# A Strassen-style gated MLP in six groups of weight chunks: 3, 4, 4, 4, 4, 3 instead of 2, 4, 4, 4, 4, 4, with new orders on ScalarE and VectorE

## The chip, the cores and the metric

The kernel runs on one core of one Trainium2 chip. The metric is the device time of one execution in microseconds. Before the change it is 1894.84 us, the median of 3 runs (1894.76 to 1895.4). All times below are microseconds unless marked ns.

## The reference, cut to what matters

The program is one inference step of a two-layer encoder over 656 tokens: 16 meta tokens, 512 prompt frames and 8 x 16 sample frames. Each layer has a token mixer (left untouched here) and then the channel mixer, in float32:

```python
def conv_ffn(h, p, buf):
    u = h @ p['w_ffn_up']                      # 1024 -> 2 x 2816
    a, v = u[..., :D_FF], u[..., D_FF:]
    ext = jnp.concatenate([buf.astype(a.dtype), a], axis=1)
    c = p['ffn_conv_b'] + sum(ext[:, j:j + T] * w[j] for j in range(CONV_W))
    out = (jax.nn.silu(c) * v) @ p['w_ffn_down']   # 2816 -> 1024
    return out, ext[:, -(CONV_W - 1):]
```

Its output is normalised (RMSNorm) and added to x, and the next layer begins with another norm.

## The kernel before, in words

Tokens lie along the free dimension (656 = 2 halves of 328), channels on the 128 partitions. D_FF = 2816 makes 22 chunks of 128 channels, c0 to c21. Every float32 product is done as three matmuls of 328 columns, on operands split in a high and a low part. ScalarE (ACT) makes the high part of a piece of weights (whi), VectorE (DVE) the low part (wlo, whi subtracted from the raw weights); both also do all the elementwise work, and each runs strictly in the order that is written for it.

**Plain chunks.** Chunks 0 to 2 (NPL = 3) compute a and v as ordinary tiles. TensorE (PE) computes tiles T_UP to T_UP + 5; on DVE `plain_a`, `conv_rest`, `plain_v` and `g_low` turn them into the gated product g, split in gh and gl. Meanwhile ACT and DVE form the sums of activations that the Strassen chunks need: Sh/Sl and part of Hh/Hl (`s_sum`, `s_high`, `s_low`).

**Strassen chunks.** Chunks 3 to 21 use seven products each (B11, B21, T2, T3, T1, T4, B22) of 12 matmuls (`chunk`, L928 on PE, L1970 on ACT, L2773 on DVE). ACT copies partial results out of PSUM: p1 after B11, u2 after T2, p7 after T3. T2 needs p1 taken, T1 needs u2 taken, T4 needs p7 taken, and B22 needs DVE's addition of T1 to p7 (`dve_took`). Beside its own products, the chunk's ACT and DVE orders finish the previous chunk, called pending: `conv_first`, `conv_rest`, `silu`, `times_v`, `g_high`, `g_low`. In the last group `times_v` also multiplies by R.

**Down passes.** GROUPS (L65) says after which chunks a down pass comes. A pass over a group of nk chunks (`down_pass`, L977) computes 8 output tiles n, each nk blocks of 6 matmuls, in three PSUM banks (G0, WB, G1). For n = 0 to 2 it first runs all blocks but those of the last chunk. In the first pass ACT copies the tiles to Y; in later ones DVE adds them to Y. The last pass runs n = 3 to 7 in halves of the tokens, all first halves first, so that the norm of the first half can begin (`norm_sum_a`).

**The weight stream.** Pieces of 512 KB are loaded by SP's queue into four slots (`raw_slot`, L257; wraw holds 0 and 1, wff 2 and 3), each once the piece that held the slot has been split. The Strassen sums of weights T1 to T4 are made by GpSimd's (POOL's) accumulating DMAs (L731 to L760), in one order: within a group T1 of chunk c + 1 is issued ahead of T4 of chunk c. T1 of c + 1 waits for that chunk's v piece to be loaded, T4 of c for the split of B21 of c. Split weights go into a ring of three full slots; `split_after` (L502) lists, for each product or piece of the stream (a unit), which splits may be made once it has been computed, and `highs(l, u)` (L1581) and `lows(l, u)` (L2259) make all those that are listed up to unit u. T4 and B22 are mostly split as one pair.

Of the kernel before, what the change touches and what calls it, by code (L numbers as in the profile page):

```python
# [18 lines left out]
ALU = mybir.AluOpType  # L19
# [5 lines left out]
KD = D // P  # L25
# [15 lines left out]
KF = FF // P  # L41
# [20 lines left out]


NPL = 3
GROUPS = [(0, 2), (2, 6), (6, 10), (10, 14), (14, 18), (18, KF)]  # L65
NQ = len(GROUPS)
NS = KF - NPL
G4 = 4
# [6 lines left out]

def group_of(c):
    return next(q for q, (c0, c1) in enumerate(GROUPS) if c0 <= c < c1)

# [27 lines left out]
def build(nc, a):  # L108
# [6 lines left out]
    with ctx:  # L115
# [126 lines left out]
        def chunk_no(l, c):  # L242
            return l * NS + c - NPL
# [11 lines left out]
            return u if q is None else P_PASS[q] + u - U_PASS[q]  # L255

        def raw_slot(p):  # L257
            return p % 2 if p < P_UP + 2 * NPL else p % 4

        def raw_of(p):  # L260
            return wraw[:, p % 2, :] if raw_slot(p) < 2 else wff[:, p % 2, :]

        def last_unit(p):

# [236 lines left out]

        split_after = {}  # L502
        _i = P_UP + 2 * NPL - 1
        for _u in range(U_PROD[NPL], UNITS_L):
            _w, _k = max(users[UNITS_L + _u]) - UNITS_L, product_of(_u)
            if _k and product_of(_w):
                _w += LATE[_k[1]]
            _i = max(_i, _w)
            split_after.setdefault(_i, []).append(_u)
# [71 lines left out]
        def _(sp):  # L581
# [32 lines left out]
            for g in range(DEPTH * PIECES):  # L614
# [28 lines left out]
                p = g % PIECES  # L643
                if earlier[g] is not None:
                    sp.wait_ge(S("w_split"), earlier[g] // PIECES * UNITS_L + last_unit(earlier[g] % PIECES) + 1)
                if p == P_CHUNK[NPL]:
                    sp.wait_ge(S("oas_taken"), l + 1)
                    sp.wait_ge(S("ob_split"), HG * (l + 1))
                    sp.wait_ge(S("out"), 32 * (l + 1))
# [147 lines left out]
        def _(pe):  # L797
# [130 lines left out]
            def chunk(l, c):  # L928


                j, s, q = chunk_no(l, c), c % 2, group_of(c)
                x_, y_, z_ = bank(G[s], 0), bank(G[s], 1), bank(WA, s)
                lo, hi = slice(0, KH), slice(KH, KD)
                a_, b_ = cols_of(0), cols_of(1)
# [533 lines left out]
        def _(act):  # L1468
# [13 lines left out]
            def f(*args, **kw):  # L1482
                prev()
                return act.activation(*args, **kw)  # L1484
# [108 lines left out]
            for l in range(DEPTH):  # L1593
# [376 lines left out]
                def chunk(c, pending):  # L1970


                    u0, s = U_PROD[c], c % 2

                    def after(i):
                        act.wait_ge(S("product"), product_no(l, c, i))

                    if pending is not None:
                        conv_first(pending)
                        carry(pending)  # L1980
                    highs(l, u0 - 1)
                    after(B11)
                    act.wait_ge(S("ax"), l * KF + c)
                    did(f(p1, bank(G[s], 0), ACT.Copy), "act_took")
                    highs(l, u0 + B11)
                    if pending is not None:
                        silu(pending)
                    halo(c)
                    highs(l, u0 + B21)
                    after(T2)  # L1990
                    did(f(u2, bank(G[s], 0), ACT.Copy), "act_took")
                    highs(l, u0 + T2)
                    if pending is not None:
                        g_high(pending)
                    after(T3)
                    act.wait_ge(S("gl"), 2 * (l * KF + c) - 1)
                    did(f(p7[:, :], bank(WA, s), ACT.Copy), "act_took")
                    highs(l, u0 + T1)
                    highs(l, u0 + T4)

                for q, (c0, c1) in enumerate(GROUPS):
                    for c in range(max(c0, NPL), c1):
                        chunk(c, c - 1 if c > max(c0, NPL) else None)
                    last_c, u0, nk = max(c1 - 1, NPL - 1), U_PASS[q], c1 - c0
                    if q:
                        conv_first(last_c)
                        carry(last_c)
                        highs(l, u0 - 1)
                        silu(last_c)
                    else:  # L2010
                        highs(l, u0 - 1)
                    g_high(last_c)
                    if q == NQ - 1:
                        w_high(l, UNITS_L - 1)
                    for n in range(KD):
                        if not q:
                            act.wait_ge(S("down"), down_no(l, q, n))
                            did(f(two(Y[:, n, :]), halves(down_bank(n)), ACT.Copy), "act_took")
                        if not q and n == 3:
                            s_high(Sh[:, 0, :, :], Sf[:, 0, :, :], 18)  # L2020
                            act.wait_ge(S("tile"), t0 + T_UP + 2 * NPL)
                            for x in range(2):
                                s_high(Hh[:, 2 * x:2 * x + 2, cols_of(1)], s4_part(x), 12, -1.0)
                        if q < NQ - 1 and nk * (n + 1) % 8 == 0:
                            highs(l, u0 + nk * (n + 1) // 8 - 1)
                exp_table()
                split_to[0] = 0
# [82 lines left out]
                    act.dma_start(a["o_conv"][l], cout[:, :, :]).then_inc(S("conv_out"), 16)  # L2110
                else:
                    rstd_post_a(2 * l + 2)
                    square(0, 0)
                    square(0, 1)
                    for n in (3, 4):
                        ffn_out_b(n)
                        scale_y(n, 1)
                    ffn_out_b(KD - 3)
                    scale_y(KD - 3, 1)
                    ffn_out_b(KD - 2)  # L2120
                    scale_y(KD - 2, 1)
                    ffn_out_b(KD - 1)
                    square(0, 2)
                    square(0, 3)
                    rstd_post_b(2 * l + 2)
# [23 lines left out]
        def _(dve):  # L2149
# [173 lines left out]
            for l in range(DEPTH):  # L2323
# [398 lines left out]
                def times_v(c):  # L2722
# [5 lines left out]
                    if group_of(c) == NQ - 1:  # L2728
                        step(tt_(d, d, R[:, :], ALU.mult))
                    dve.wait_ge(S("product"), product_no(l, c, B22))  # L2730
                    did(stt(d[:, cols_of(0)], bank(G[c % 2], 0), -1.0, d[:, cols_of(0)], ALU.mult, ALU.mult), "dve")
                    did(stt(d[:, cols_of(1)], p7[:, :], -1.0, d[:, cols_of(1)], ALU.mult, ALU.mult), "gl")

                def s_low(i, to, src, hi_, scale=1.0):
# [26 lines left out]
                plain_v(1)  # L2761
                plain_a(2)
                w_low(l, P_UP + 6)
                g_low(1)
                conv_rest(2)
                plain_v(2)
                w_low(l, P_UP + 7)
                for k in range(KH):
# [3 lines left out]

                def chunk(c, pending):  # L2773

                    u0, s = U_PROD[c], c % 2
                    s_ = ax[:, c % 2, :]

                    def after(i):
# [2 lines left out]
                    lows(l, u0 - 2)  # L2781
                    if pending is not None:
                        conv_rest(pending)
                    lows(l, u0 + B11)
                    after(B21)
                    dve.wait_ge(S("act_took"), act_took(l, c, 0))
                    step(tt_(s_[:, 2:2 + HALF], bank(G[s], 1), p1, ALU.add))
# [117 lines left out]
                rest(1, 6)  # L2905
                rest(1, 7)

            residual(0, 0)
            residual(0, 1)
            ffn_out_b(4)  # L2910
            add_square_b(n0 + N_FFNPOST, 3)
            residual(0, 2, 2)
            add_square_b(n0 + N_FFNPOST, 4)
            ffn_out_b(KD - 3)
            residual(0, 4, 2)
            ffn_out_b(KD - 2)
            add_square_b(n0 + N_FFNPOST, KD - 3)
            residual(0, 6, 2)
            add_square_b(n0 + N_FFNPOST, KD - 2)
            ffn_out_b(KD - 1)  # L2920
            add_square_b(n0 + N_FFNPOST, KD - 1)
            dve.wait_ge(S("rstd"), n0 + N_FFNPOST + 1)
            residual(1, 0)
            residual(1, 1)
# [135 lines left out]
```

## Time and profile before

| | us |
|---|---|
| median of 3 runs | 1894.84 |
| the profiled execution, its own time | 1895.83 |
| its span, first to last instruction | 1894.0 |
| PE busy with matmuls | 1807.6 (95%) |
| DVE busy | 1267.4 (67%) |
| ACT busy | 952.9 (50%) |
| POOL busy | 230.2 (12%) |
| mean granted clock of TensorE | 0.985 |

The profile page gives busy times and the span in 40 slices; the trace gives every instruction with its start, what it waited for and its length. A busy PE is not PE at its peak: matmuls overlap, and their ends are modelled. The span is 1.8 us shorter than the execution's own time, which is 1.0 us above the median.

### The profile page before, as it was taken

Reading aid. Unit: us, or ns where it says so; the run is one execution under the profiler, and the core shown is the slowest. Engines: PE = TensorE matmul, PEld = TensorE weight load, DVE = VectorE, ACT = ScalarE, POOL = GpSimd, SP = SyncE. Lnnn points to the kernel's source line nnn. Section 1 sums busy time; section 2 is a strip of 40 time slices with the busy share of each in tenths; the row PEclk is TensorE's granted clock in tenths of the full one; section 3 lists DMA queues with packets and bytes.
Section 4 is the critical chain, followed back from the end, with each engine's and each line's share of the span. In section 5 each row is a group of like instructions: output and inputs, shape, how many; then the busy total and the mean of one; then the engine's idle time right before and its main releaser. Section 6 shows DMA issues by size and latency. Waiting matters only on the chain.

```text
span 1894.0 us, 31220 instructions
## 1 busy us (share of the span) xinstructions
PE 1807.6 (95%) x11636; PEld 1656.5 (87%) x11636; DVE 1267.4 (67%) x1973; ACT 952.9 (50%) x1593; POOL 230.2 (12%) x257
## 2 busy tenths in 40 slices
PE   8999999999999999999899999999998999999995
PEld 7999976598999999999799999657988999999984
DVE  5777875536775756778767778654377766757776
ACT  6444546435663544535654444554375443535355
POOL 0000023200112121111000000340001121111100
PEclk9999999999999999999999999999999999999998
DMA  5312121411556666656131122313125675666631
GB/s 183 91 58 69 63 74 45 164 39 56 126 134 152 162 153 156 146 156 156 34 108 47 58 69 73 80 56 128 57 60 145 156 162 134 159 158 164 143 74 62
DMA packets 98902, 204.03 MB, mean 108 GB/s; under 512 B 16864, under 2 KB 35680, under 8 KB 98728
## 3 DMA queue, kind: packets, MB, share of 16 engines
q1 hardware_dynamic: 63952, 144.39, 23.8%
q0 software_dynamic: 21888, 39.86, 12.8%
q10 hardware_dynamic: 12912, 17.78, 2.8%
q8 instruction: 94, 1.54, 0.3%
q14 instruction: 56, 0.46, 0.1%
HBM read 170.98 MB, written 8.65 MB: 95 GB/s over the span
## 4 chain that ended last, share of the span: by engine, by line
PE 61%; DVE 18%; ACT 9%; issue 6%; DMA 5%; POOL 1%; DVEq 0%; ACTq 0%; SPq 0%; POOLq 0%
PE G L799 38%; PE WA L799 13%; PE WB L799 8%; DVE wlo L2166 4%; DVE tmp L2166 2%; DMA wraw<-t 2%; ACT whi L1484 2%; DVE cc L2166 2%; DMA t<-in_wstream 2%; PE G L803 1%; DVE Y L2166 1%; DVE ax L2166 1%; PE WB L803 1%; ACT sq L1484 1%; DVE X L2166 1%
## 5 line engine op out<-in xcount | busy, mean ns | idle before, releaser
L799 PE MATMUL G<-Hh,wlo 128*128 128x328 f32 x1384 | 451.9, 327 | 11.8 <-DVE Hl L2166 8.2
L799 PE MATMUL G<-Hh,whi 128*128 128x328 f32 x1384 | 435.5, 315 | 0.0
L799 PE MATMUL G<-Hl,whi 128*128 128x328 f32 x1384 | 434.2, 314 | 0.0
L799 PEld LDWEIGHTS G<-Hh,wlo 128*128 128x128 f32 x1384 | 263.1, 190 | 23.1 <-DVE Hl L2166 11.8
L799 PEld LDWEIGHTS G<-Hh,whi 128*128 128x128 f32 x1384 | 263.1, 190 | 2.4 <-issue 0.6
L1484 ACT ACTIVATE whi<-wraw 128x1024 fp32r<-128x1024 f32 (+2 forms) x171 | 155.8, 911 | 213.6 <-PE G L799 117.9
L799 PEld LDWEIGHTS G<-Hl,whi 128*128 128x128 f32 x1384 | 262.7, 190 | 0.0
L2166 DVE TENSOR_TENSOR wlo<-wraw,whi 128x1024 fp32r<-128x1024 f32 (+2 forms) x171 | 177.5, 1038 | 72.7 <-ACT whi L1484 61.1
L799 PE MATMUL G<-gh,wlo 128*128 128x328 f32 x424 | 134.2, 317 | 7.1 <-DVE tmp L2166 6.2
L799 PE MATMUL G<-gh,whi 128*128 128x328 f32 x424 | 132.7, 313 | 0.0
L799 PE MATMUL G<-gl,whi 128*128 128x328 f32 x424 | 132.1, 312 | 0.0
L2166 DVE TENSOR_TENSOR wlo<-wff,whi 128x1024 fp32r<-128x1024 f32 (+1 forms) x85 | 86.0, 1012 | 40.0 <-ACT whi L1484 34.5
L1484 ACT ACTIVATE whi<-wff 128x1024 fp32r<-128x1024 f32 (+1 forms) x85 | 75.8, 892 | 55.7 <-PE WB L799 33.0
L799 PE MATMUL G<-Sh,wlo 128*128 128x328 f32 x304 | 96.1, 316 | 5.2 <-ACT R L1484 5.2
L799 PE MATMUL G<-Sl,whi 128*128 128x328 f32 x304 | 95.1, 313 | 0.0
L799 PE MATMUL G<-Sh,whi 128*128 128x328 f32 x304 | 95.0, 312 | 0.0
L2166 DVE SCALAR_TENSOR_TENSOR cc<-ax,cols,cc 128x672 f32<-128x672 f32 x88 | 80.9, 919 | 18.4 <-ACT cc L1484 16.3
L799 PE MATMUL WB<-gh,wlo 128*128 128x328 f32 x248 | 79.7, 321 | 11.8 <-ACT Y L1484 11.8
L799 PEld LDWEIGHTS G<-gh,wlo 128*128 128x128 f32 x424 | 79.8, 188 | 10.9 <-DVE tmp L2166 9.6
L799 PE MATMUL WA<-Hh,wlo 128*128 128x328 f32 x216 | 69.5, 322 | 11.4 <-ACT p L1484 11.4
L2166 DVE TENSOR_TENSOR Y<-Y,G 128x656 f32<-128x656 f32 (+1 forms) x56 | 42.9, 765 | 55.4 <-PE G L799 52.8
L799 PEld LDWEIGHTS G<-gl,whi 128*128 128x128 f32 x424 | 79.7, 188 | 0.0
(327 smaller groups left out, 4084.9 us busy)
## 6 DMA issues: line engine op xcount, KB each, us to landing
wraw<-in_wstream SPq DMA_DIRECT2D x108, 512.0 KB, 3.4
wff<-in_wstream SPq DMA_DIRECT2D x40, 512.0 KB, 4.8
t<-in_wstream SPq DMA_DIRECT2D x76, 256.0 KB, 4.7
t<-in_wstream POOLq DMA_DIRECT2D x38, 256.0 KB, 4.4
ckT<-in_ckT SPq DMA_DIRECT2D x12, 512.0 KB, 3.4
wff<-in_wstream POOLq DMA_DIRECT2D x20, 256.0 KB, 4.4
t<-wff POOLq DMA_DIRECT2D x20, 256.0 KB, 3.3
wff<-t POOLq DMA_DIRECT2D x20, 256.0 KB, 4.2
```

The source lines that it names most:

```text
L799: return pe.matmul(out, lhsT, rhs, start=start, stop=stop, skip_group_check=True)
L803: return pe.transpose(out, in_, ident[0:n, 0:n])
L1484: return act.activation(*args, **kw)
L2166: return kind(*args, **kw)
```

## The change

It moves the borders of the groups, so that the first pass takes all three plain chunks and the last one three Strassen chunks instead of four; PSUM sides and weight slots are counted so that they fit. It also moves some calls in the orders of ACT and DVE: in `chunk` the split that may follow B11 (L1985, L2784) comes with the next call of `highs` or `lows` instead, and on ACT the p7 copy goes ahead of `g_high`; in the first pass ACT's `s_high` stands at n = 5 instead of 3; and the final tail of the last layer is reordered.

```diff
-GROUPS = [(0, 2), (2, 6), (6, 10), (10, 14), (14, 18), (18, KF)]
+GROUPS = [(0, 3), (3, 7), (7, 11), (11, 15), (15, 19), (19, KF)]
...
+def side(c):
+
+    return (c - GROUPS[group_of(c)][1]) % 2
...
         def raw_slot(p):
-            return p % 2 if p < P_UP + 2 * NPL else p % 4
+            return p % 2 if p < P_UP + 2 * NPL else (p - P_UP - 2 * NPL) % 4 if p < P_CHUNK[NPL] else (p - P_CHUNK[NPL]) % 4
...
         split_after = {}
         _i = P_UP + 2 * NPL - 1
-        for _u in range(U_PROD[NPL], UNITS_L):
+        for _u in range(P_UP + 2 * NPL + 2, UNITS_L):
...
-                if p == P_CHUNK[NPL]:
+                if p == P_UP + 2 * NPL + 2:
...
-                j, s, q = chunk_no(l, c), c % 2, group_of(c)
+                j, s, q = chunk_no(l, c), side(c), group_of(c)
...
                     did(f(p1, bank(G[s], 0), ACT.Copy), "act_took")
-                    highs(l, u0 + B11)
                     if pending is not None:
                         silu(pending)
                     halo(c)
...
                     highs(l, u0 + T2)
-                    if pending is not None:
-                        g_high(pending)
                     after(T3)
                     act.wait_ge(S("gl"), 2 * (l * KF + c) - 1)
                     did(f(p7[:, :], bank(WA, s), ACT.Copy), "act_took")
+                    if pending is not None:
+                        g_high(pending)
                     highs(l, u0 + T1)
...
-                        if not q and n == 3:
+                        if not q and n == 5:
                             s_high(Sh[:, 0, :, :], Sf[:, 0, :, :], 18)
...
-                        if q < NQ - 1 and nk * (n + 1) % 8 == 0:
+                        if q and q < NQ - 1 and nk * (n + 1) % 8 == 0:
+                            highs(l, u0 + nk * (n + 1) // 8 - 1)
+                        if not q and n >= 5:
                             highs(l, u0 + nk * (n + 1) // 8 - 1)
...
                     rstd_post_a(2 * l + 2)
-                    square(0, 0)
-                    square(0, 1)
                     for n in (3, 4):
                         ffn_out_b(n)
                         scale_y(n, 1)
+                    square(0, 0)
                     ffn_out_b(KD - 3)
                     scale_y(KD - 3, 1)
                     ffn_out_b(KD - 2)
+                    square(0, 1)
+                    ffn_out_b(KD - 1)
                     scale_y(KD - 2, 1)
-                    ffn_out_b(KD - 1)
...
                 w_low(l, P_UP + 6)
+                conv_rest(2)
                 g_low(1)
-                conv_rest(2)
...
                     if pending is not None:
                         conv_rest(pending)
-                    lows(l, u0 + B11)
                     after(B21)
...
+            ffn_out_b(4)
             residual(0, 0)
+            add_square_b(n0 + N_FFNPOST, 3)
+            ffn_out_b(KD - 3)
             residual(0, 1)
-            ffn_out_b(4)
-            add_square_b(n0 + N_FFNPOST, 3)
+            add_square_b(n0 + N_FFNPOST, 4)
+            ffn_out_b(KD - 2)
             residual(0, 2, 2)
-            add_square_b(n0 + N_FFNPOST, 4)
-            ffn_out_b(KD - 3)
+            add_square_b(n0 + N_FFNPOST, KD - 3)
+            ffn_out_b(KD - 1)
+            add_square_b(n0 + N_FFNPOST, KD - 2)
             residual(0, 4, 2)
-            ffn_out_b(KD - 2)
-            add_square_b(n0 + N_FFNPOST, KD - 3)
+            add_square_b(n0 + N_FFNPOST, KD - 1)
             residual(0, 6, 2)
-            add_square_b(n0 + N_FFNPOST, KD - 2)
-            ffn_out_b(KD - 1)
-            add_square_b(n0 + N_FFNPOST, KD - 1)
```

## Rows read from the trace of the kernel before

**Rows 1.** The page: PE's busy time, and its granted clock in 40 slices.

```profile
PE 1807.6 (95%) x11636; PEld 1656.5 (87%) x11636; DVE 1267.4 (67%) x1973; ACT 952.9 (50%) x1593; POOL 230.2 (12%) x257
...
PEclk9999999999999999999999999999999999999998
```

**Rows 2.** Timeline of PE, first pass, layer 0: start, length, operation, [idle before, releaser].

```profile
508.41 0.42 PE L799 MATMUL G<-gh,wlo 128*128 128x328 f32 x1 [0.95 <-DVE tmp L2166]
...
525.33 0.64 PE L799 MATMUL WB<-gh,wlo 128*128 128x328 f32 x1 [5.87 <-ACT Y L1484]
...
528.77 0.41 PE L799 MATMUL G<-Hh,wlo 128*128 128x328 f32 x1
```

**Rows 3.** Timeline of ACT in the same stretch.

```profile
514.11 0.72 ACT L1484 ACTIVATE Y<-G 128x656 f32<-128x656 f32 x1 [1.00 <-PE G L799]
520.29 1.30 ACT L1484 ACTIVATE Sh<-Sf 128x1312 fp32r<-128x1312 f32 x1 [5.46 <-DVE Sf L2166]
```

**Rows 4.** Timeline of DVE in the same stretch.

```profile
507.51 0.84 DVE L2166 TENSOR_TENSOR tmp<-G,tmp 128x656 f32<-128x656 f32 x1 [1.05 <-ACT tmp L1484]
...
515.67 0.84 DVE L2166 TENSOR_TENSOR gl<-tmp,gh 128x656 fp32r<-128x656 f32 x1
...
517.91 2.35 DVE L2166 SCALAR_TENSOR_TENSOR Sf<-X,cols,Sf 128x328 f32<-128x328 f32 x4
521.62 1.52 DVE L2166 TENSOR_TENSOR Sl<-Sf,Sh 128x1312 fp32r<-128x1312 f32 x1 [1.36 <-ACT Sh L1484]
523.26 0.84 DVE L2166 SCALAR_TENSOR_TENSOR Hl<-gh_f,Hh 128x656 fp32r<-128x656 f32 x1
```

**Rows 5.** The line that issues the T4 sums, L760: issue to landing.

```profile
DMA to landing us min/median/max: 3.3/4.9/6.8
```

**Rows 6.** Timelines of DVE, SP, POOL, ACT around chunks 7 and 8, layer 0.

```profile
612.38 1.23 DVE L2166 TENSOR_TENSOR wlo<-wff,whi 128x1024 fp32r<-128x1024 f32 x1 [0.38 <-ACT whi L1484]
...
613.64 0.80 SPq L651 DMA_DIRECT2D wff<-in_wstream  x2
...
620.85 1.23 POOL L760 DMA_DIRECT2D wraw<-t  x1
...
626.27 1.38 ACT L1484 ACTIVATE whi<-wraw 128x512 fp32r<-128x512 f32 x2 [2.51 <-DMA wraw<-t]
627.76 0.99 ACT L1484 ACTIVATE tmp<-cc 128x528 f32<-128x528 f32 x2
...
629.10 0.44 ACT L1484 ACTIVATE R<-G 128x328 f32<-128x328 f32 x1
```

**Rows 7.** Waits of PE (us, times, longest): whole span, 850 to 897, 1780 to 1828.

```profile
PE WA L799 <- ACT p L1484: 11.4, 12, 1.8
...
PE G L799 <- ACT R L1484: 5.2, 6, 1.3
...
PE WA L799 <- ACT p L1484: 2.8, 3, 1.3
...
PE WA L799 <- ACT p L1484: 3.9, 3, 1.8
```

**Rows 8.** Timeline of PE in the last group's chunks, layer 1.

```profile
1792.38 0.31 PE L799 MATMUL G<-Sh,whi 128*128 128x328 f32 x1
1792.53 0.31 PE L799 MATMUL G<-Sl,whi 128*128 128x328 f32 x1
...
1796.19 0.47 PE L799 MATMUL WA<-Hh,whi 128*128 128x328 f32 x1
```

**Rows 9.** Timelines of PE and DVE in the last pass, layer 0.

```profile
902.74 0.42 PE L799 MATMUL G<-gh,wlo 128*128 128x328 f32 x1 [1.21 <-DVE tmp L2166]
...
906.66 0.84 DVE L2166 TENSOR_TENSOR Y<-Y,G 128x656 f32<-128x656 f32 x1 [0.75 <-PE G L799]
...
922.95 0.54 PE L799 MATMUL WA<-acc,ones 128*128 128x328 f32 x1 [1.05 <-DVE acc L2166]
```

**Rows 10.** Timeline of DVE in the final tail.

```profile
1870.82 0.50 DVE L2166 TENSOR_TENSOR tmp<-Y,R 128x328 f32<-128x328 f32 x1 [2.63 <-ACT R L1484]
```

More of the change, by code:

```diff
@@ L257, in raw_slot @@
         def raw_slot(p):
-            return p % 2 if p < P_UP + 2 * NPL else p % 4
+            return p % 2 if p < P_UP + 2 * NPL else (p - P_UP - 2 * NPL) % 4 if p < P_CHUNK[NPL] else (p - P_CHUNK[NPL]) % 4
         def raw_of(p):
-            return wraw[:, p % 2, :] if raw_slot(p) < 2 else wff[:, p % 2, :]
+            s = raw_slot(p)
+            return wraw[:, s, :] if s < 2 else wff[:, s - 2, :]
         def last_unit(p):
@@ L1970, in chunk @@
                 def chunk(c, pending):
-                    u0, s = U_PROD[c], c % 2
+                    u0, s = U_PROD[c], side(c)
                     def after(i):
@@ L2730, in times_v @@
                     dve.wait_ge(S("product"), product_no(l, c, B22))
-                    did(stt(d[:, cols_of(0)], bank(G[c % 2], 0), -1.0, d[:, cols_of(0)], ALU.mult, ALU.mult), "dve")
+                    did(stt(d[:, cols_of(0)], bank(G[side(c)], 0), -1.0, d[:, cols_of(0)], ALU.mult, ALU.mult), "dve")
                     did(stt(d[:, cols_of(1)], p7[:, :], -1.0, d[:, cols_of(1)], ALU.mult, ALU.mult), "gl")
@@ L2773, in chunk @@
                 def chunk(c, pending):
-                    u0, s = U_PROD[c], c % 2
+                    u0, s = U_PROD[c], side(c)
                     s_ = ax[:, c % 2, :]
```

## The prediction

> **What bounds the kernel now.** I read the page first, then PE's waits, then the timelines around each of them. PE is busy for 1807.6 of 1894.0 us and holds the higher clock nearly everywhere [rows 1]. At it a matmul starts every 0.15 us, after a lapse every 0.27 [rows 8]. So a Strassen product is 1.8 us, a chunk 12.6, a block of a down pass 0.9. The change adds or takes no matmul: it carries 8 blocks, 7.2 us of PE work, from the last pass of each layer to the first. What counts is where PE waits, place by place.
>
> Before, each first pass has a stall of 5.9 us: PE wants PSUM bank WB again, which ACT has not copied [rows 2], since at n = 3 ACT stood 5.46 us at `s_high`, waiting for DVE's sums [rows 3]. DVE is the late one. After the stall twelve matmuls take 3.44 us (525.33 to 528.77) instead of 1.8: 1.6 us for the lapse of the clock. Later, PE waits for ACT's u2 copy (ACT R, 5.2 us in 6 places) and p7 copy (ACT p, 11.4 in 12 places, 6.7 of it in the last groups) [rows 7]. In the last pass DVE and ACT are the bound: PE waits for DVE at its start and its middle [rows 9].
>
> **The first pass (layer 0; layer 1 is alike).** The last plain tile ends at 505.5: 508.41 less 0.95 idle, 0.3 of modelled end and 1.8 of blocks, plus 0.15 [rows 2]. With nk = 3 PE has 6 x 0.9 = 5.4 us of blocks of chunks 0 and 1, to 510.9; the wait of 0.95 for DVE's `plain_v(2)` is covered. Then it needs gh and gl of chunk 2. But `g_low(2)` stands behind four weight sums and two `s_low` in DVE's order, which the change doesn't touch: it ends at 515.67 + 0.84 = 516.5 [rows 4]. The swap of `conv_rest(2)` and `g_low(1)` can bring `plain_v(2)`, which now waits 1.05 for ACT, forward by 0.1 or so, since the tile itself ends just before. I take 516.4: a stall of 5.5 us, plus 1.6 for the clock. The rest of the pass is 18 blocks, 16.2 us, so it ends at 534.2, against 528.8.
>
> Now ACT's `s_high` stands behind the copy of tile 5, which PE ends at 534.2 - 5.4 = 528.8, though DVE's sums are ready at 517.91 + 2.35 = 520.3 [rows 4]. From 528.8: copy 0.8, `s_high` 1.4, DVE's `s_low` 1.6, its two Hl 1.9, and then the low part of the B11/B21 pair 1.3 [rows 3, 4, 6]: 7.0. That pair stood ahead of all this before; now its ring slots come free with the first piece of the pass, and DVE's `lows` has it after n = 7. So B11 of chunk 3 starts at 535.8, a stall of 1.6. Worse, the T4 sum of chunk 3 can only be issued when B21 is split, also at 535.8, and ACT has T4's split ahead of the p1 copy for which T2 waits. With 5.2 us to landing (between the median 4.9 and the 5.4 from 620.85 to 626.27), 0.7 for the high part and 0.6 for the copy, T2 starts at about 542.5, not at 539.5: 3.0 us [rows 5, 6]. Before, T2 started at 528.8 + 3.6 = 532.4. The region costs **+10.1 us** in layer 0, of which 7.2 is the work carried in; in layer 1 I take 9.9. Bounds: 8 with the shortest landing, 12 with a long one. A lapse of the clock behind the 3.0 us wait costs 1.6 more; one followed a wait of 1.8 [rows 7, 8], so I take it as likely: **+2.2** for both layers. Sum +22.2.
>
> The transfer is where the Trainium skill gives another result. The traced landings are 3.3 to 6.8 us for 256 KB [rows 5]. The page DMA: Bandwidth & Descriptors (Anatomy of one DMA — SWDGE (gpsimd) path) fits 2.0 us plus bytes/436e3 per such transfer, 2.6 us here; by it T4 would land in time almost everywhere and the sum would be that of the first rival below, or less. The trace doesn't agree: its shortest is 3.3.
>
> **Third chunks of a group (c5, c9, c13, c17; before c8, c12, c16).** Here T4 waits in POOL's order behind T1 of the next chunk, and that one for a load which waits for the split of the T4/B22 pair one chunk earlier. Before: the pair's low part ends at 613.6, SP loads, T4 is issued at 620.85, ACT has it at 626.27, then splits, does `silu` and a small copy, and takes u2 at 629.10 [rows 6]. The change has two effects. ACT does `silu` before the split, so u2 comes 1.5 after T4's landing, not 2.8: 1.3 gained. But DVE's low part moves behind `silu`, the addition of ax and `times_v`: by the lengths in rows 6 and two pairs of 0.5 us operations, 2.3 later; and so the load, T1 and T4. Net, u2 is 1.0 later: T1's wait is 0.9 (5.2 / 6) + 1.0 = 1.9. The loads meet fewer other transfers, 0.4 less by my estimate: 1.5. The p7 wait there ((11.4 - 6.7) / 6 = 0.8) goes, and B22 waits some 0.4 for DVE, whose p7 addition is behind a later `g_low`. Each wait costs 0.25 more than its idle time (modelled end and slow first matmul). Before: 5.2 + 4.7 + 12 x 0.25 = 12.9; after: 8 x (1.9 + 0.2) = 16.8. **+3.9.** Bounds: -12.9 if every T4 is early enough, +13 more if the clock lapses each time.
>
> **Chunks of the last group.** Before, p7 waits behind `g_high`, which waits for `times_v` with its extra multiplication: 6.7 us in 6 places, with 1.5 for the restarts and about 2.1 for one lapse [rows 7, 8]. After, p7 needs `times_v` only, which now has no split ahead of it; I count its end about 0.5 before T3's. The queue behind it, `g_high` and `g_low`, delays the p7 addition by 0.1 to 0.2. Only 2 chunks have a pending one. 10.3 becomes 0.6: **-9.7** (bounds -10.3 and -5).
>
> **The last pass.** Before it starts at 896.0 (902.74 less 1.2, 0.3 and 5.25) and the first half's norm matmul comes at 922.95, released by DVE: 27.0 us [rows 9]. Two blocks each of n = 0 and 1 cover 3.6 us instead of 5.4, so the bank wait of 1.2 grows to about 2.9. But DVE's chain ends this stretch: its first Y addition waits for PE by 0.75, then for the rest; it can start 0.75 sooner, and nothing behind it shrinks. So of 7.2 us of PE work taken out only **0.75** comes back in each layer (bounds 0 and 2). The one split less after B22 lies in DVE's idle time. What follows to the next layer is DVE's as well.
>
> **The final tail.** Now `residual(0, 6, 2)`, about 1.9 us, stands behind the last square addition, and so lies in DVE's wait of 2.63 for the norm [rows 10]. I take **-2.0** (bounds 0 and -3).
>
> Sum: 22.2 + 3.9 - 9.7 - 1.5 - 2.0 = +12.9 on 1895.8, the profiled execution's time; less the 1.0 by which that stands above the median, **1908 us** (1907.7). Fewer loads per layer (runs of 384 columns, 64 instead of 71) and some lone splits in place of pairs cost nothing: no wait ends on them.
>
> **Rivals.** (1) T4 in time: landing 3.3 us after issue, the shortest seen, instead of 5.2. T1 of the third chunks wouldn't wait (-8 x 1.6), chunk 3's T2 would wait 1.9 less (-3.8), with no lapse (-2.2): 1889, on the faster side. It decides from a landing about 5.2 us after the third chunk's start. For it: SP may load faster where less else runs. Against it: the rows show 5.4 for this very sum. Chance 0.12. (2) The wider first pass swallows DVE's lag, that is, `g_low(2)` is there in time: 7.1 us less in each layer, 1894, no change. Against it: the end at 516.5 read above, and an order that isn't touched. Chance 0.11. (3) The clock lapses after each third chunk's wait too: 8 x 1.6 = 13 more, 1921. For it: one lapse after a wait of 1.8; against it: none after the other waits of rows 7. Chance 0.08. The forecast has 0.69. That the change doesn't do what it says I exclude: the groups are a table that everything reads.
>
> **The range** takes in the bounds of the first pass and of the third chunks partly met: 1891 to 1917 leaves out most of rivals 1 and 3. A measurement of this kernel can tell about 0.2%, 3.8 us, from no change. Faster (rival 1 and a part of the low bounds) 0.15, same 0.12, slower 0.73.
>
> **What the new profile would show.** In the first pass one PE wait for DVE gl of some 5 us, none for ACT Y, and a second for ACT's copy at T2 of chunk 3. From the last plain tile to that T2 37 us instead of 27. Third chunks: waits for ACT R of 1 to 2 us, POOL's T4 issue 1.5 us or more after the chunk's start; few waits for ACT p in the last group. Last pass: some 26 us to the norm matmul. The prediction is wrong if the gl wait is under 3 us, or if u2 is in time in the third chunks.

## The result, and the profile after

The kernel after takes 1901.72 us, the median of 7 runs (1898.38 to 1903.4), against 1894.84 (1893.31 to 1895.65, 7 runs). The ratio is 1.0033, 95% interval 1.0021 to 1.0044: 4 to 8 us slower. Forecast were 13 us more. The sign was right, the size about twice too large; the forecast range, 1891 to 1917, holds the result.

The profiled execution took 1898.38 us (span 1896.6), 2.6 more in span than the one of before (1894.0). It is the fastest of its 7, the median is 3.3 above it; a part of that gap is looked at below. PE's work is the same [rows 1]:

```profile
PE 1808.2 (95%) x11636; PEld 1654.2 (87%) x11636; DVE 1265.0 (67%) x1970; ACT 950.8 (50%) x1592; POOL 230.2 (12%) x257
...
PEclk9999999999999999999999999999999999999998
```

PE's waits over the whole span (us in total, times, longest). ACT p, 11.4 in 12 places before [rows 7], is gone from the list, and ACT R falls from 5.2 to 2.1. DVE gl is new (10.7: twice 5.2), and DVE tmp, 6.2 before, is 10.3.

```profile
PE G L805 <- DVE gl L2173: 10.7, 3, 5.2
PE G L805 <- DVE tmp L2173: 10.3, 10, 2.9
...
PE G L805 <- ACT Y L1490: 3.4, 2, 1.7
...
PE G L805 <- DVE p L2173: 2.5, 9, 0.3
...
PE G L805 <- ACT R L1490: 2.1, 2, 1.3
```

**The first pass.** Timeline of PE, layer 0, in the places of [rows 2]: the wait for g_low(2), B11 of chunk 3, T2 of chunk 3.

```profile
516.08 0.61 PE L805 MATMUL G<-gh,wlo 128*128 128x328 f32 x1 [5.17 <-DVE gl L2173]
...
536.56 0.39 PE L805 MATMUL G<-Hh,wlo 128*128 128x328 f32 x1 [1.72 <-ACT Y L1490]
...
541.59 0.39 PE L805 MATMUL G<-Sh,wlo 128*128 128x328 f32 x1 [1.21 <-issue]
```

DVE in the same stretch [rows 4]: g_low(2) ends at 515.94 (forecast 516.4), and `s_low` waits 11.97 for ACT's `s_high`.

```profile
515.10 0.84 DVE L2173 TENSOR_TENSOR gl<-tmp,gh 128x656 fp32r<-128x656 f32 x1
...
531.62 1.53 DVE L2173 TENSOR_TENSOR Sl<-Sf,Sh 128x1312 fp32r<-128x1312 f32 x1 [11.97 <-ACT Sh L1490]
...
535.19 1.23 DVE L2173 TENSOR_TENSOR wlo<-wraw,whi 128x1024 fp32r<-128x1024 f32 x1
```

POOL issues T4's sum of chunk 3, ACT splits it and copies p1:

```profile
536.71 0.86 POOL L766 DMA_DIRECT2D wraw<-t  x1 [10.43 <-DVE wlo L2173]
```

```profile
540.30 0.63 ACT L1490 ACTIVATE whi<-wraw 128x512 fp32r<-128x512 f32 x1 [2.28 <-DMA wraw<-t]
541.04 0.44 ACT L1490 ACTIVATE R<-G 128x328 f32<-128x328 f32 x1
```

The order of events is the forecast one, with two lengths off. The lower clock behind the wait for g_low(2) lasts longer than forecast: 18 matmuls, 516.08 to 521.14, start 0.27 apart and take 5.06 us instead of 2.7, so the lapse costs 2.4 (2.1 in layer 1), not 1.6. And it is 3.6 us from T4's issue to ACT, not 5.2. PE's gap at T2 is 1.4 us beyond its beat of 0.15, not 3.0, and the twelve matmuls behind it hold the higher clock.

**A third chunk.** Chunk 9, layer 0, one period later than chunk 8 in [rows 6]: DVE's low part of the pair, SP's load, POOL's T1 and T4, ACT's split and u2 copy.

```profile
638.86 1.23 DVE L2173 TENSOR_TENSOR wlo<-wff,whi 128x1024 fp32r<-128x1024 f32 x1
```

```profile
640.11 0.80 SPq L657 DMA_DIRECT2D wff<-in_wstream  x2
```

```profile
645.15 0.87 POOL L742 DMA_DIRECT2D wff<-in_wstream  x1 [7.88 <-DMA wff<-in_wstream]
645.69 1.23 POOL L766 DMA_DIRECT2D wraw<-t  x1
```

```profile
650.74 1.06 ACT L1490 ACTIVATE whi<-wraw 128x1024 fp32r<-128x1024 f32 x1 [0.76 <-DMA wraw<-t]
651.89 0.45 ACT L1490 ACTIVATE R<-G 128x328 f32<-128x328 f32 x1
```

The SP line is two loads of 512 KB; T1's sum waits for the second. T4 goes 5.6 us after the first of them is issued; before it took 7.2 (613.64 to 620.85, [rows 6]). The chunk's first matmul is at 645.36, so T4 is issued 0.3 us after it and lands at 650.66, 5.3 after it. T1 of this chunk does not wait. Of the eight third chunks only chunk 5 of layer 0 and chunk 17 of layer 1 waited over 0.2 us for ACT R (0.75 and 1.33); there T4 landed 6.4 and 7.0 us after the chunk's first matmul. The prediction named u2 in time in the third chunks as a sign that it is wrong, and in six of eight it is in time.

**The last pass.** PE waits 2.88 at its start (forecast 2.9), and the norm's matmul comes at 927.99. From the pass's start that is 26.2 us in layer 0 (27.0 before, [rows 9]) and 24.9 in layer 1 (24.7 before).

```profile
908.45 0.42 PE L805 MATMUL G<-gh,wlo 128*128 128x328 f32 x1 [2.88 <-DVE tmp L2173]
...
927.99 0.82 PE L805 MATMUL WA<-acc,ones 128*128 128x328 f32 x2 [2.39 <-DVE acc L2173]
```

**The account of the two profiles**, in us:

| stretch, both layers | forecast | measured |
|---|---|---|
| last plain tile to T2 of chunk 3 | +22.2 | +18.6 (9.5, 9.1) |
| from there to the last pass | -5.8 | -8.4 (-3.3, -5.2) |
| last pass to the norm's first matmul | -1.5 | -0.6 (-0.8, +0.2) |
| final tail, between the norm's two matmuls | -2.0 | -2.7 |
| same stretch in layer 0, mixer, end | 0 | -4.0 |

The last row I put down to the clock. Between the norm's two matmuls of layer 0 the profile after has 22.2 us and the one before 24.1. Over all 17 kernels profiled here this stretch takes 22.2 us where the clock is at its lower level for 0 or 3.4 us of it (8 kernels), 22.8 to 23.1 where for 4.8 to 6.5 (5 kernels; a sixth has 23.1 with 8.7), and 24.1 where for 8.3 to 8.6 (3 kernels). The stretch behind it, to the first down block of layer 1 and mostly the mixer, takes 483.8 us in the profile after, with no time at the lower level, and 486.4 in the one before, with 8.6 us of it (-2.6); all 17 lie between. The end varies from 25.0 to 26.4 (+0.5 here). That the new groups have no part in where the clock falls isn't shown: the mixer's mean is 484.5 in the 7 kernels with new groups and 485.6 in the 10 with old ones. Lines of the windows view, columns: stretch, length, busy times, clock, DMA share, GB/s, of after and then of before.

```profile
928.00:951.00 23.00, 16.30 (x79) 13.75 (x80) 17.84 (x28) 14.17 (x27) 0.00 (x0) 0.93 0.14 47
```

```profile
923.00:948.00 25.00, 19.53 (x87) 16.23 (x87) 17.84 (x28) 14.11 (x25) 0.00 (x0) 0.81 0.13 43
```

Without the last row the profiles differ by 6.9 us (the first four rows), as the medians do (6.9); -0.4 of the span's difference of 2.6 lies ahead of the first row.

### The profile page after: what moved, and what is told of

Read it like the earlier page. It is cut to its first block, busy times and chain, and to the rows that moved or that the text cites. A ratio compares the mean times of both kernels' runs of the same rounds, so it can differ in the third digit from the quotient of the medians.

```text
span 1896.6 us, 31198 instructions
## 1 busy us (share of the span) xinstructions
PE 1808.2 (95%) x11636; PEld 1654.2 (87%) x11636; DVE 1265.0 (67%) x1970; ACT 950.8 (50%) x1592; POOL 230.2 (12%) x257
## 3 DMA queue, kind: packets, MB, share of 16 engines
q0 software_dynamic: 21888, 39.86, 12.9%
## 4 chain that ended last, share of the span: by engine, by line
PE 57%; DVE 18%; ACT 11%; issue 6%; DMA 5%; POOL 1%; DVEq 0%; ACTq 0%; SPq 0%; POOLq 0%
PE G L805 35%; PE WA L805 12%; PE WB L805 8%; DVE wlo L2173 4%; ACT whi L1490 2%; DVE cc L2173 2%; DMA t<-in_wstream 2%; DVE tmp L2173 2%; DMA wraw<-t 1%; PE G L809 1%; ACT sq L1490 1%; DVE Y L2173 1%; ACT R L1490 1%; ACT cc L1490 1%; DVE gl L2173 1%
## 5 line engine op out<-in xcount | busy, mean ns | idle before, releaser
L805 PE MATMUL G<-Hh,wlo 128*128 128x328 f32 x1384 | 453.2, 327 | 18.6 <-DVE Hl L2173 7.9
L805 PE MATMUL G<-gh,wlo 128*128 128x328 f32 x420 | 135.1, 322 | 23.0 <-DVE gl L2173 10.7
L742 POOL DMA_DIRECT2D wraw<-in_wstream x20 | 17.5, 875 | 592.2 <-DMA wraw<-in_wstream 592.2
L805 PEld LDWEIGHTS G<-gh,whi 128*128 128x128 f32 x420 | 80.7, 192 | 0.0
```

Of the source, the lines that this page charges most:

```text
L742: pool.dma_start(v[:, 0:W_HALF], a["wstream"][l, S_UP[c // FH] + 2 * (c % FH)][:, 0:W_HALF], accum_op=ALU.add).then_inc(S("T1"), 16)
L805: return pe.matmul(out, lhsT, rhs, start=start, stop=stop, skip_group_check=True)
```

## The experiments

Ratios are to the kernel before, run beside each on the same chip; they differ by up to 0.0006 from the ratios of the medians. Names that begin with a are edits of the kernel after, with b of the kernel before.

**1. The new groups with the old orders in a chunk** (a_groups_old_chunk_orders).

```diff
                     did(f(p1, bank(G[s], 0), ACT.Copy), "act_took")
+                    highs(l, u0 + B11)
...
+                    if pending is not None:
+                        g_high(pending)
                     after(T3)
...
+                    lows(l, u0 + B11)
                     after(B21)
```

> The kernel after, with the orders inside a Strassen chunk put back (split behind B11 on ACT and DVE, g_high ahead of the p7 copy). Theory A, the groups cost time and the orders win it back: the waits for p7 return (in the kernel before 4.7 us in 6 places outside the last group; in the last groups 1.1 us in each chunk with a pending one, of which 4 are left instead of 6), with 0.25 us each for the restart, while the growth of the waits at the start of the passes (0.38 to 0.73 us, 8 times) goes: +6.2 + 5.4 - 2.8, so 9 us above the kernel after, 1.008 of the kernel before. Theory B, the orders are neutral or a loss (the late splits delay T4's sum, as the prediction had it) and only p7 gains in the last groups: within 4 us of the kernel after, and T4's landing no earlier than in it.

Measured: 1.0089 (1.0077 to 1.0102), 1911.6 us, 10 above the kernel after. Theory A holds for the orders together; which of the two it is comes in experiment 11. The groups with `s_high` and the tail cost 17 us; the chunk's orders win 10 of it back. ACT p is there again:

```profile
PE WA L805 <- ACT p L1490: 13.5, 14, 2.0
...
PE G L805 <- ACT R L1490: 6.3, 8, 1.5
```

**2. g_low(2) ahead of the sums** (a_gl2_early).

```diff
                 w_low(l, P_UP + 7)
+                g_low(2)
                 for k in range(KH):
                     s_sum(s4_part(k // 2)[:, k % 2, :], KH + k, 0, Sf[:, 1, k, :])
...
                     else:
-                        g_low(last_c)
                         lows(l, u0 - 1)
```

> The kernel after, with g_low(2) moved ahead of the weight sums and s_low in the first pass. Theory A, the place of g_low(2) is what the first pass pays: the wait of 5.2 us for gl goes with its restart (0.25) and the lapse of the clock behind it (1.6), in both layers: 14 us less than the kernel after, 0.996 of the kernel before; the waits at B11 (1.9) and T2 (1.4) of chunk 3 stay, since they hang on tile 5. Theory B, DVE is only late by its whole work there: the sums that are now later by 0.84 us delay s_high and the low parts, and the waits at B11 and T2 of chunk 3 grow by what the first one loses: less than 5 us gained.

Measured: 0.9963 (0.995 to 0.9977), 13 us less than the kernel after. Theory A, to 1 us: one operation's place made the new groups slower than before. The wait for gl is 0.21 now, those at B11 and T2 of chunk 3 stand as expected:

```profile
511.93 0.40 PE L805 MATMUL G<-gh,wlo 128*128 128x328 f32 x1 [0.21 <-DVE gl L2173]
...
530.05 0.39 PE L805 MATMUL G<-Hh,wlo 128*128 128x328 f32 x1 [1.71 <-ACT Y L1490]
...
535.10 0.39 PE L805 MATMUL G<-Sh,wlo 128*128 128x328 f32 x1 [1.23 <-issue]
```

**3. Only p7 ahead of g_high** (b_p7_first).

```diff
-                    if pending is not None:
-                        g_high(pending)
                     after(T3)
...
                     did(f(p7[:, :], bank(WA, s), ACT.Copy), "act_took")
+                    if pending is not None:
+                        g_high(pending)
```

> The kernel before, with only the p7 copy put ahead of g_high on ACT. Theory A: the 12 waits for ACT p (11.4 us) go with 0.25 us each for restarts, and 0.4 us return as waits of B22 in some 12 chunks: 9 to 11 us less than the kernel before, 0.995, and 1.6 more where the lapse in the last group goes. Theory B, g_high then ends too late and g_low with it, so that the pass that waits for gl or the next chunk's addition starts later: under 4 us gained, and new waits of PE for gl or DVE p as long as those removed.

Measured: 0.999 (0.9981 to 0.9999). Theory A falls. ACT p loses 8.4 us, and DVE p (4.0), DVE tmp (+2.2) and ACT R (+2.0) take them up:

```profile
PE G L799 <- DVE tmp L2166: 8.4, 12, 1.5
PE G L799 <- ACT R L1484: 7.2, 6, 1.6
...
PE G L799 <- DVE p L2166: 4.0, 13, 0.4
PE WA L799 <- ACT p L1484: 3.0, 5, 1.1
```

**4. Only the late split** (b_split_late).

```diff
                     did(f(p1, bank(G[s], 0), ACT.Copy), "act_took")
-                    highs(l, u0 + B11)
...
-                    lows(l, u0 + B11)
                     after(B21)
```

> The kernel before, with only the split behind B11 left to the next call of highs or lows on ACT and DVE. The prediction's step (theory B): T4's sum is issued 2.3 us later in each third chunk and u2 is taken 1.0 later, +1.0 to 1.5 in each of 8: 8 to 12 us slower. Theory A, read from the profile after: with T3's sum out of the way the load and T1's sum take 5.0 us instead of 6.7, so T4 lands as before, ACT's silu no longer stands behind its landing, and the u2 waits (5.2 us in 6 places) mostly go, while the waits at the start of 8 passes grow by 0.35 each: between 4 us less and the same as the kernel before.

Measured: 0.9962 (0.995 to 0.9974), 7 us less, better than either theory. It is the term that the prediction had as a loss. Times of the two kernels must be taken from the chunk's own start, since chunk 8 begins 0.8 us earlier with the late split. First matmul of chunk 8, before and with the late split:

```profile
621.31 0.31 PE L799 MATMUL G<-Hh,wlo 128*128 128x328 f32 x1
```

```profile
620.49 0.31 PE L799 MATMUL G<-Hh,wlo 128*128 128x328 f32 x1
```

The pair's low part now ends at 615.17 instead of 613.61, 5.3 us ahead of the chunk's start instead of 7.7, and the load follows it: 2.4 later, as forecast. But T4 is issued 0.2 after the chunk's start, where it was 0.5 ahead of it, so only 0.7 later. And ACT, its `silu` done before T4 has landed, takes u2 6.9 after the start instead of 7.8. DVE, SP, POOL and ACT with the late split:

```profile
613.94 1.23 DVE L2165 TENSOR_TENSOR wlo<-wff,whi 128x1024 fp32r<-128x1024 f32 x1
```

```profile
615.19 0.80 SPq L651 DMA_DIRECT2D wff<-in_wstream  x2
```

```profile
620.70 1.22 POOL L760 DMA_DIRECT2D wraw<-t  x1
```

```profile
623.80 0.99 ACT L1484 ACTIVATE tmp<-cc 128x528 f32<-128x528 f32 x2 [0.87 <-DVE cc L2165]
...
625.94 1.38 ACT L1484 ACTIVATE whi<-wraw 128x512 fp32r<-128x512 f32 x2 [0.91 <-DMA wraw<-t]
627.41 0.44 ACT L1484 ACTIVATE R<-G 128x328 f32<-128x328 f32 x1
```

The means over all third chunks, from each chunk's first matmul; two rows are of the kernel after and of experiment 5:

| | loads issued | from there to T1's sum | T4 issued | T4 landed | u2 taken | T1 waits |
|---|---|---|---|---|---|---|
| before (6 chunks) | -7.6 | 6.6 | -0.3 | 5.0 | 7.8 | 0.9 |
| late split (6) | -5.3 | 5.4 | 0.7 | 5.7 | 7.1 | 0.3 |
| after (8) | -5.2 | 5.3 | 0.7 | 5.9 | 7.1 | 0.3 |
| T3's sum small (6) | -7.6 | 5.2 | -1.8 | 4.0 | 6.7 | 0.2 |

`times_v` too has no split ahead of it, and ACT p falls from 11.4 to 5.9 with p7 still behind `g_high`.

**5. Why the load is quicker: T3's sum made small** (b_t3_small). The sum takes 8 of 512 columns (the 2048 in the expectation are bytes of a partition), and the rest of T3 is not summed in this kernel.

```diff
-                pool.dma_start(t3[:, :], a["wstream"][l, ...][:, 0:W_HALF],
+                pool.dma_start(t3[:, 0:8], a["wstream"][l, ...][:, 0:8],
```

> The kernel before with POOL's T3 sum cut from 2048 to 8 columns (the rest of T3 is then not summed; the work of PE, ACT and DVE is as before). In the kernel before the load of chunk 9's v piece is issued at 613.64 and T1's sum can go at 620.31, 6.7 us later; in the kernel after and with the late split it takes 5.0. The low part that gates it ends at 613.61. Theory A, the T3 sum, issued at 611.6, slows the load: without it the load takes 5.0 to 5.5 us here too, T4 is issued 1.2 to 1.7 earlier and the waits for ACT R (5.2 us in 6 places) mostly go, 4 to 7 us gained. Theory B, the load is slow for another reason (T3's or T4's own first load, SP's order): it still takes 6.5 us or more and the time is within 2 us of before.

Measured: 0.9951 (0.9933 to 0.9969), 9 us less. Theory A, with more gained than its 4 to 7. The loads of 612.80 let T1's sum go at 617.82, after 5.0 us instead of 6.7 (means 5.2 and 6.6), with the old order of splits, and ACT R falls from 5.2 to 1.7. The lines of POOL and SP:

```profile
610.75 0.87 POOL L750 DMA_DIRECT2D t<-in_wstream  x1 [1.85 <-DMA t<-in_wstream]
617.82 0.87 POOL L736 DMA_DIRECT2D wff<-in_wstream  x1 [6.20 <-DMA wff<-in_wstream]
618.36 1.22 POOL L760 DMA_DIRECT2D wraw<-t  x1
```

```profile
612.80 0.80 SPq L651 DMA_DIRECT2D wff<-in_wstream  x2
```

In the kernel before the T3 sum is issued at 611.60, 2.0 us ahead of the load; in the late split 3.6 ahead (611.63, 615.19). That sum lands at 616.10 and 615.77. So the loads overlap with it for 2.5 us in the one kernel and 0.6 in the other, and of 2.3 us that they start later, 1.2 to 1.3 are back when T1's sum goes (table above). The small sum also takes load off every other transfer, so the experiment shows what T3's sum costs, not that the overlap alone does it.

**6. Both chunk orders on the old groups** (b_chunk_orders: edits 3 and 4).

> The kernel before with both changes inside a Strassen chunk (late split, p7 first). Alone they gave 7 and 2 us. Theory A, they add up or better, since the late split frees DVE's low part ahead of times_v and with it g_high: the p7 waits left by the late split (5.9 us in 13 places) and their restarts turn into waits of B22 of 0.1 to 0.3: 9 to 12 us less than the kernel before, ratio 0.994 to 0.995. Theory B, both act on the same waits: 7 us, 0.996.

Measured: 0.9983 (0.9974 to 0.9993). Neither theory: a smaller gain than that of the late split alone (0.9962, measured on another chip; the intervals touch). PE now waits for DVE instead: DVE tmp 9.5 (5.9 with the late split alone) and DVE p 4.1 (0.7), for the 5.9 of ACT p.

**7. s_high at n = 5 alone** (b_shigh5), with the splits of the first pass from n = 5 on.

```diff
-                        if not q and n == 3:
+                        if not q and n == 5:
```

> The kernel before, with only ACT's s_high in the first pass put at n = 5 instead of 3 (and the splits of the pass from n = 5 on). The wait for WB (5.9 us) goes with its restart and the lapse behind it (1.6). Theory A, DVE's sums are what is late: they end at 520.3 whatever ACT does, then s_high 1.4, s_low 1.5, two Hl 1.9 give B11 of chunk 3 at 525 where PE would be ready at 521: about 4 us of the 7.7 come back at B11 or T2, so 3 to 4 us gained in each layer, 1887 to 1889, ratio 0.996. Theory B, all of it is gained: 15 us, 0.992. Theory C, the stall is only moved to B11: no change.

Measured: 0.9981 (0.9971 to 0.999), 3 to 4 us in all, half of theory A. The 5.9 us at WB are gone and 3.7 come back at T2 of chunk 3, where ACT has splits and two late Y copies ahead of p1. The lapse of the clock comes along: behind T2 20 matmuls start 0.27 apart, to 532.87 (12 in layer 1).

```profile
527.26 0.61 PE L799 MATMUL G<-Sh,wlo 128*128 128x328 f32 x1 [3.68 <-ACT R L1484]
```

**8. The final tail alone** (b_tail: the tail's hunks of the change, on ACT and DVE).

> The kernel before with the final tail's new order alone. Both theories: from the norm's matmul of the second half of layer 1 to the end 2.2 us less, as in the profile after; ratio 0.999. If the tail's gain was another's (an earlier start of DVE there), it is 1.000 and the tail's length in the trace is as before.

Measured: 0.9983 (0.997 to 0.9996). Between the norm's two matmuls of layer 1, 13.0 us instead of 15.8. From the second one to the end, where the expectation had placed the gain, nothing is gained (26.2 us, 25.8 before). The second one waited 7.64 before and waits 4.14 now:

```profile
1863.48 1.46 PE L799 MATMUL WA<-acc,ones 128*128 128x328 f32 x2 [4.14 <-DVE acc L2166]
```

**9. The new orders on the old groups** (b_orders_all: edits 3, 4, 7 and 8; of the change's orders only the swap of `conv_rest(2)` and `g_low(1)` is left out).

> The kernel before with every new order of the change and the old groups and slots, so that its difference to the kernel after (1901.7) is the groups alone. Sum of the parts: chunk orders -9 to -12, s_high at n = 5 -7, final tail -2: 1874 to 1877, ratio 0.990. Theory A: the groups alone cost 25 us or so. Theory B, the parts overlap: above 1883.

Measured: 0.9939 (0.9925 to 0.9952), 1883.8 us. That is 12 us less than before. It is short of the sum expected (theory B by its number), but not because these parts overlap: as measured in experiments 6, 7 and 8 they give 3.2, 3.6 and 3.2, together 10. What fell short are the pair of chunk orders (9 to 12 expected) and `s_high` (7). Against the kernel after (1.0033) the new groups, with that swap, cost 18 us, of which experiment 2 gives 13 back.

**10. T4 ahead of T1 on POOL** (a_gl2_t4_first, on top of experiment 2).

```diff
+                    third = c == GROUPS[group_of(c)][0] + 2
-                    if within:
+                    if within and not third:
                         sum_t1(l, c + 1)
                     sum_t4(l, c)
                     if c + 1 < KF:
-                        if not within:
+                        if third or not within:
                             sum_t1(l, c + 1)
```

> The kernel after with g_low(2) early (1888.1), and POOL issuing T4's sum of each third chunk of a group ahead of T1's sum of the next one. Theory A, the order on POOL is what makes T4 late and so the source of the u2 waits (5.0 us in 6 places in that kernel's trace) and of the spread between runs: T4 lands 4 us or more earlier, the u2 waits go, 5 to 7 us gained, 1881 to 1883, with a spread below 3 us. Theory B, the two sums then change places: T1 of the fourth chunk lands late and PE waits for it as long. Theory C, T4 waits for the split of B21 in any case: nothing changes.

Measured: 1.0 (0.9986 to 1.0013), 7 us slower than experiment 2, and the spread is wider (11 us in 11 runs against 8 in 7). Theory B, and worse: PE waits at T2 of the fourth chunk instead, in five of eight, up to 4.1 us:

```profile
1504.72 0.42 PE L806 MATMUL G<-Sh,wlo 128*128 128x328 f32 x1 [4.06 <-ACT R L1491]
```

**11. p7's place in the new groups** (a_p7_old: the kernel after with g_high ahead of p7 again).

> The kernel after with g_high ahead of the p7 copy again, the late splits kept. Both orders together are worth 10.7 us in these groups. Theory A, the prediction's: p7's place is the larger part, since p7 waited for g_high: 5 us or more slower than the kernel after (1907 or more, 1.006 of the kernel before). Theory B, as the runs on the old groups show: with the late split times_v and g_high are early enough, the p7 wait left is 0.3 to 0.5 in a chunk with a pending one (13 or so), and it is paid back by waits at the passes' starts that are 0.35 shorter (8) and B22 waits of 0.2 less: within 2 us of the kernel after.

Measured: 1.002 (1.0009 to 1.0031), if anything below the kernel after. Theory B. With experiment 1 (1.0089) this puts the whole gain of the chunk's orders in the new groups on the late split: 13 us for it, nothing for p7. DVE tmp is 6.7 here, 10.3 in the kernel after:

```profile
PE G L805 <- DVE tmp L2173: 6.7, 10, 2.5
PE WA L805 <- ACT p L1490: 4.9, 8, 0.8
```

**12. and 13. Chunk 3's p1 copy ahead of the splits** (b_c3_p1_first, on experiment 9, with `s_high` at n = 6), and the same with g_high ahead of p7 (b_c3_p1_first_p7_old).

```diff
-                    highs(l, u0 - 1)
+                    if c > NPL:
+                        highs(l, u0 - 1)
                     after(B11)
```

> The old groups with all new orders (0.9939 of before), and in chunk 3 ACT's p1 copy ahead of the two splits that stood before it, s_high at n = 6. In that kernel's trace PE waits 3.9 us at T2 of chunk 3 for p1, which ACT takes at 527.6 though B11 ended at 522; DVE's low part for T2 ends at 526.1. Theory A, ACT's order makes that wait: it becomes 1.9 or less: 2 us less in each layer, and 1.6 more where the clock does not lapse: ratio 0.990 to 0.992. Theory B, what stood before p1 is then late for T1 or T4: no change, 0.994.

> The run before this one with g_high ahead of the p7 copy again. Theory A, p7 first is a loss once the split is late (late split alone 0.9962, both 0.9983, in runs of two calls): 2 to 4 us less than the run before this one, the waits at the start of 8 passes back from 0.7 to 0.3 us, p7 waits of 0.3 to 0.5. Theory B, that difference was chance: the two within 1 us.

Measured: 0.9943 (0.9929 to 0.9958) and 0.9927 (0.991 to 0.9944). The first says theory B: T2 of chunk 3 waits 1.9 instead of 3.7 (the pass's own `highs` still has one split ahead of p1), but T2 of chunk 4 now waits 2.7, with a lapse of the clock behind it:

```profile
526.64 0.39 PE L799 MATMUL G<-Sh,wlo 128*128 128x328 f32 x1 [1.92 <-ACT R L1484]
...
542.25 0.64 PE L799 MATMUL G<-Sh,wlo 128*128 128x328 f32 x1 [2.73 <-ACT R L1484]
```

The second is 3 us lower, but the intervals overlap.

**14. The new groups at their best** (a_best: experiments 2, 11 and 12's edit, `s_high` at n = 4).

> The new groups at their best: the kernel after with g_low(2) early, g_high ahead of p7, s_high at n = 4, and in chunk 3 the p1 copy ahead of the splits that stood before it. Against the kernel with g_low(2) early alone (0.9963 of before): B11's wait for s_high (1.9) and T2's (1.4) go in both layers, 6 us with restarts; p7's place 0 to 3. Theory A: 0.992 to 0.993, 1880 to 1882. Theory B, DVE's two Hl and the low part behind s_high end late whatever ACT does (their length is 4.7 us): B11 or T2 waits as before, 0.996.

Measured: 0.9935 (0.9914 to 0.9956), near theory A. In layer 0 the wait at B11 is gone and T2 of chunk 3 waits 2.5 for T4's sum; in layer 1 B11 waits 1.2 and T2 not at all. It can't be told from experiment 13 (1879.1 and 1878.0 us): with both ordered well, no gain of the groups of 3, 4, 4, 4, 4, 3 over 2, 4, 4, 4, 4, 4 shows. The two are 0.65 and 0.73% faster than the kernel before.

**15. The kernel after again** (after_again).

> The kernel after once more, for its spread. Its 7 runs lay between 1898.4 and 1903.4 while its profiled run, 1898.4, had few waits for u2 (ACT R 2.0 us in 2 places). Theory A, T4's sum lands with a margin of only 0.3 us in the third chunks, so a second profile shows other chunks late: in a run near the median of 1901.7, 2 to 4 us more of waits for ACT R, with one or two waits over 1.5 us and a lapse behind one. Theory B, the spread comes from lapses of the clock elsewhere (mixer, front): the waits for ACT R are 2 us again.

Measured: 1899.8 us (1898.05 to 1906.45), 1.0032 (1.002 to 1.0043). Its profiled run, at the median, waits 1.8 us for ACT R in 2 places, so this profile speaks for theory B. The differences of 2.6 us in the mixer and 1.9 between the norm's two matmuls of layer 0 are of the size of the spread. That T4's landing takes part in other runs isn't excluded: in experiment 2's profile ACT R is 5.0, in 6 places, with no edit near it.

## Why the prediction was right or wrong

**First pass, +10.1 and +9.9 per layer:** right in every event, measured 9.5 and 9.1. The stall for g_low(2) was 5.2 with a lapse of 2.4 and 2.1 behind it (forecast 5.5 and 1.6), the one at B11 1.9 (1.6). Experiment 2 shows the stall and its lapse alone at 13 us for both layers. The wait at T2 of chunk 3 was 1.4 for a forecast of 3.0: the landing was taken as 5.2 us from the rows of chunk 8, where T1's sum is issued 0.5 us ahead of T4's. Chunk 3's T4 has no such neighbour and took 3.6. In the 17 profiles it lands in 3.3 to 3.6 us 33 times of 34, and in 5.4 the one time that T1's sum was 0.7 us ahead (experiment 14, layer 0).

**+2.2 for a lapse behind that wait:** wrong, with the wait. 1.4 us of gap had no lapse.

**Third chunks, +3.9:** this is the step that failed. Measured about -4: from the distances of matmul starts, T1, T4 and B22 of these chunks lose 13.2 us before (forecast 12.9) and 9.2 after (16.8). I had the low part "2.3 later; and so the load, T1 and T4", less 0.4 by estimate. The low part and the load are 2.3 later, but T4 is issued only 1.1 later and lands 0.7 later (experiment 4's table): the path from the load to the landing is 1.6 us shorter, not 0.4, since the load that ran into T3's sum hardly does any more (4 and 5). The other half, `silu` ahead of the split, was right with its 1.3. So u2 came 0.7 earlier instead of 0.6 later, and T1 waits 0.3 instead of 1.5. B22's waits were rightly seen: 4.2 us for these chunks with their restarts (forecast 8 x 0.4 without). There is also a slip in the sum: with 0.25 for each of the two waits, 16.8 would have been 19.2. The p7 waits fell in part for a reason that I gave to the other edit (11.4 to 5.9 by the late split alone).

**Last group, -9.7:** measured about -8.7, so right in size. But the text gave it to p7's place and to the late split together, and by experiment 11 p7's place has no part in it in the new groups: the three last chunks lose 1.3 us with either. On the old groups (experiment 3) the B22 waits take up about half of what it frees there.

**A term that I had at zero:** the wait at the start of a pass, for DVE's `times_v`, grew from 0.4 to 0.7 us beyond PE's beat at each of the 8 middle passes, and with B22's waits outside the third chunks came to some +4. Experiment 11, with g_high ahead of p7 again, takes the growth away. This loss hides half of the error in the third chunks: that the total is off by 6 us and not by 10 is luck.

**Last pass, -0.75 per layer:** right that almost nothing comes back. Of 7.2 us of PE work less in each layer, 0.8 came back in layer 0 and nothing in layer 1 (+0.2); in the profile of experiment 15 nothing in either. **Final tail, -2.0:** -2.7, shown alone in experiment 8.

**The rivals.** (1) T4 in time: its premise, a landing 3.3 us after issue, came true for chunk 3 (3.6) and not in the third chunks, where T4 lands 4.6 to 6.2 us after its issue. Its outcome came true there too in six of eight, since T4 is issued 0.7 us after the chunk's start on average, where I had 1.5 or more. It was to decide "from a landing about 5.2 us after the third chunk's start"; chunk 9's came at 5.3 with no wait, and landings up to 5.8 cost 0.14 at most. I had set its chance at 0.12. The Trainium skill's page that I weighed (DMA: Bandwidth & Descriptors, Anatomy of one DMA — SWDGE (gpsimd) path) gives, as an estimate from its fit, 2.6 us for a 256 KB transfer; the landings after are 3.6 to 6.7, with a median of 5.5, so the trace still disagrees. (2) and (3) didn't happen: g_low(2) was late, and in the profile after no lapse followed a third chunk's wait.

What stays open: why both chunk orders together gave 3 us on the old groups and 10 on the new ones, and how far the spread of the runs comes from T4.

## What to carry to other kernels

When a split or copy is moved later, follow the transfer behind it to its landing, not only to its issue: a load that starts 2.3 us later, after a busy stretch of the queues, let the last sum behind it land only 0.7 later. Compare such times from the chunk's own start, since the whole kernel shifts. Work taken from an engine that isn't the bound of a stage and carried to one where it is comes out as a cost of its full size; before moving it, ask what the receiving stage lacks (here one operation of 0.84 us, which stood behind 5.7 us of sums). And of two edits that remove the same wait, run each alone: one may hold the whole gain.

## What the runs showed of the hardware

A pair of 512 KB loads, the second issued 0.4 us behind the first, released T1's sum 6.6 us after its issue where a 256 KB accumulating transfer had been issued 2.0 us ahead of it (mean of six third chunks, before), after 5.4 with that transfer 3.7 us ahead (experiment 4), and after 5.2 with it cut to 8 of 512 columns (experiment 5).

An accumulating transfer of 256 KB within the core's memory, T4 of chunk 3, landed in 3.3 to 3.6 us in 33 of 34 cases, and in 5.4 in the one with another accumulating transfer issued 0.7 us ahead.

Behind a stall of 5.2 us the clock stayed at its lower level for 18 matmuls (16 in layer 1) that start 0.27 us apart instead of 0.15, behind one of 5.9 us for 12: the longer stall did not have the longer lapse. With the clock two other stretches moved, the mixer by up to 2.6 us and the one between layer 0's two norm matmuls by 1.9, so a profile of one execution can be off by 3 us from its kernel's median, as here.
